# Products of constants in the waits at the borders between sublayers of an encoder trunk

## The reference, cut to what matters

```python
def rmsnorm(x, gain):
    y = xf * lax.rsqrt(jnp.mean(xf * xf, axis=-1, keepdims=True) + EPS)
    return y * gain

def swiglu(h, w_in, w_out):
    gate, up = jnp.split(h @ w_in, 2, axis=-1)
    return (jax.nn.silu(gate) * up) @ w_out

x = x + 0.5 * rmsnorm(swiglu(rmsnorm(x, g[0]), ffn_w_in[l, 0], ffn_w_out[l, 0]), g[1])
...
x = x + rmsnorm(m, g[3])
```

## Time and profile before

| | us |
|---|---|
| median of 3 runs | 2142.0 (2140.52 to 2144.03) |
| the profiled execution | 2141.13 |
| its span, first to last instruction | 2139.3 |
| TensorE busy | 2062.4 (96% of the span) |
| VectorE, ScalarE, GpSimd busy | 900.7, 689.9, 664.4 |
| mean granted clock of TensorE over the span | 0.984 |

### The profile page before, as it was taken

The page is one execution under the profiler, slowest core; times in us unless marked ns, Lnnn a source line. Parts: engine busy times, 40 slices in busy tenths (PEclk is TensorE's granted clock), DMA queues, the critical chain, the costliest instruction groups (busy, mean ns, idle before and its releaser), DMA issues.

```text
span 2139.3 us, 31272 instructions
## 1 busy us (share of the span) xinstructions
PE 2062.4 (96%) x12648; PEld 1695.4 (79%) x12648; DVE 900.7 (42%) x1222; ACT 689.9 (32%) x925; POOL 664.4 (31%) x286
## 2 busy tenths in 40 slices
PE   6999999989989999998999999999999889999997
PEld 5888888767878888887888888778888778888885
DVE  4433331668454333115433311564754766333213
ACT  4222222445342222224222222453543343222221
POOL 2444444230214444441444444100000013444442
PEclk9999999999999999999999999999999999999998
DMA  4223333210122223332222333221211122222332
GB/s 148 87 90 98 96 92 97 89 50 1 59 80 89 97 89 96 98 95 85 88 94 93 96 97 95 87 71 61 71 61 60 51 69 79 98 90 97 93 100 74
DMA packets 51643, 179.61 MB, mean 84 GB/s; under 512 B 5728, under 2 KB 5984, under 8 KB 51552
## 3 DMA queue, kind: packets, MB, share of 16 engines
q1 hardware_dynamic: 51552, 178.30, 25.8%
HBM read 176.18 MB, written 2.10 MB: 83 GB/s over the span
## 4 chain that ended last, share of the span: by engine, by line
PE 93%; DVE 3%; ACT 2%; issue 1%; DMA 0%; SPq 0%; DVEq 0%; ACTq 0%
PE psum L546 28%; PE psum L547 28%; PE psum L548 27%; PE psum L782 1%; PE psum L758 1%; PE psum L886 1%; PE psum L771 1%; PE psum L632 1%; PE psum L935 1%; DVE xt L1530 0%; DVE t_a L1525 0%; DMA const<-consts 0%; PE psum L950 0%; PE psum L762 0%; PE psum L761 0%
## 5 line engine op out<-in xcount | busy, mean ns | idle before, releaser
L498 POOL TENSOR_TENSOR w_lo<-raw,w_hi 128x1024 fp32r<-128x1024 f32 (+1 forms) x282 | 664.1, 2356 | 1443.0 <-ACT w_hi L1134 1442.9
L546 PE MATMUL psum<-xg_hi,w_hi 128*128 128x512 f32 x1896 | 757.5, 400 | 39.8 <-DMA const<-consts 16.2
L547 PE MATMUL psum<-xg_lo,w_hi 128*128 128x512 f32 x1896 | 749.3, 395 | 0.2 <-issue 0.2
L548 PE MATMUL psum<-xg_hi,w_lo 128*128 128x512 f32 x1896 | 747.5, 394 | 0.0
L1134 ACT ACTIVATE w_hi<-raw 128x1024 fp32r<-128x1024 f32 (+1 forms) x339 | 350.9, 1037 | 861.6 <-DMA raw<-w_up 468.0
L546 PEld LDWEIGHTS psum<-xg_hi,w_hi 128*128 128x128 f32 x1896 | 360.0, 190 | 122.8 <-DVE xg_lo L1536 17.4
L548 PEld LDWEIGHTS psum<-xg_hi,w_lo 128*128 128x128 f32 x1896 | 359.9, 190 | 80.3
L547 PEld LDWEIGHTS psum<-xg_lo,w_hi 128*128 128x128 f32 x1896 | 360.6, 190 | 76.4 <-issue 0.7
L546 PE MATMUL psum<-hid_hi,w_hi 128*128 128x512 f32 x704 | 273.9, 389 | 0.0
L547 PE MATMUL psum<-hid_lo,w_hi 128*128 128x512 f32 x704 | 273.9, 389 | 0.0
L548 PE MATMUL psum<-hid_hi,w_lo 128*128 128x512 f32 x704 | 273.9, 389 | 0.0
(11 more groups left out here) (183 smaller groups left out, 1326.6 us busy)
## 6 DMA issues: line engine op xcount, KB each, us to landing
raw<-w_up SPq DMA_DIRECT2D x176, 512.0 KB, 3.3
raw<-w_down SPq DMA_DIRECT2D x64, 512.0 KB, 3.5
raw<-w_hgrn SPq DMA_DIRECT2D x48, 512.0 KB, 3.3
raw<-w_down SPq DMA_DIRECT2D x32, 384.0 KB, 3.2
raw<-w_mla SPq DMA_DIRECT2D x19, 512.0 KB, 3.3
xt<-x_t SPq DMA_DIRECT2D x8, 256.0 KB, 6.8
out<-xt SPq DMA_DIRECT2D x8, 256.0 KB, 2.0
sq<-positions SPq DMA_DIRECT2D x1, 256.0 KB, 9.6
```

The costliest lines, as they stand in the source:

```text
L498: pool.tensor_tensor(w_lo[slot][:, 0:n], raw[slot][:, 0:n], w_hi[slot][:, 0:n].bitcast(F32), ALU.subtract).then_inc(w_ready, 1)
L546: first = pe.matmul(ps, w_hi[slot][:, at:at + n], hi, start=start, stop=False)
L547: pe.matmul(ps, w_hi[slot][:, at:at + n], lo, start=False, stop=False)
L548: return first, pe.matmul(ps, w_lo[slot][:, at:at + n], hi, start=False, stop=stop)
```

## The change

A helper keep_clock(times) issues products of the identity (stationary) with the 256 columns of constants that hold the identity and the ones, plain f32, into bank 7. Nothing reads them. It is called with 1 between the two halves of post_statistics, with 1 before the wait for recip_made, and with 6 behind widen. The statistics at the very end get the first of these only.

```diff
+WHILE_SQUARE, WHILE_ROOT, WHILE_CHUNK = 1, 1, 6
...
+        IDLE_BANK = 7
...
                     if b == 0:
                         close(first)
+                keep_clock(WHILE_SQUARE)
                 pe.wait_ge(sq_ready, squared.next(KB))
...
+            def keep_clock(times):
+
+                for _ in range(times):
+                    pe.matmul(psum[:, IDLE_BANK, 0:2 * P], ident, const[:, 0:2 * P], start=True, stop=True)
...
             for s, (kind, _, _, _) in enumerate(SUBLAYERS):
                 if s:
                     post_statistics()
+                    keep_clock(WHILE_ROOT)
                     pe.wait_ge(recip_made, recips.next())
                     widen()
+                    keep_clock(WHILE_CHUNK)
```

## The result

| | before | after |
|---|---|---|
| median of six, us | 2141.6 (2140.1 to 2144.0) | 2130.0 (2127.6 to 2130.4) |
| ratio | | 0.9941 (95% interval 0.9931 to 0.9952) |
| profiled execution: time, span | 2141.1, 2139.3 | 2130.1, 2128.3 |

The changed kernel is 11.6 us (0.5% by the medians) faster. The forecast was 7.0 us faster, 2135.0, with a range from 2131.5 to 2140.5.

A forecast was written before the change was run, and what follows sets the result against it. TensorE was the bound, losing time at half clock at five borders. Three fifths of 8.6 us (all kept) and two fifths of 3.0 (all dropped) gave 6.4, put at 7.0: 2142.0 − 7.0 = 2135.0, range 2131.5 to 2140.5.

The forecast's parts named there:

- What bounds it: Whole kernel: TensorE, busy 96%; filling waits alone gains nothing, the loss is work at half clock behind the five borders.
- The price of a product and the three fillings: Border waits: 0.43 us a product at held clock, 0.87 otherwise; one, one and six fit, leaving 0.6 us of the third.
- What borders 2 to 5 bring when held: Borders 2 to 5 at full clock: gains of 1.8, 3.0, 1.4 and 1.8 us, 8.0 together.
- Border 1: Entry of the attention layer, bound by its chunks: only 0.2 us there and 0.46 of widening, 0.6 us if held.
- Three borders in five are kept: All five borders: the filler holds the clock at three, depending on how soon after the last wide product the drop falls due.
- The value where it falls: Borders still dropping: full clock returns sooner, worth 0.8, 0.5, 0.6 and 1.0 us at borders 2 to 5, 0 at 1.
- No DMA, no other engine's instruction and no wait moves: Program outside the fillings: the change only adds 41 products on TensorE; no term was counted for the gated layer's inside.
- The end: Last statistics: one filler product of the 41 stands there; no gain was counted for it.
- A: Rival: the clock drops at every border and only comes back sooner; 3.0 us faster, 2139.0; chance 0.14, near mixtures included.
- B: Rival: products of constants don't hold the clock and delay the real ones; 4.6 to 8.6 us slower, 2148.6; chance 0.11.
- C: Rival: all five borders kept, 8.6 us faster, 2133.4; upper part of the forecast, chance 0.70 together with it.
- D: Rival: nothing happens, as filling costs what the clock gives; within 2 us of 2142; chance 0.05.

The follow-up runs named there:

- thin: The changed kernel with each filler product cut from 256 columns to one, same instruction count: median 2141.2 us, ratio 0.9991 to the kernel before.
- twelve: The changed kernel with twelve products behind the widening in place of six: 2141.9 us, ratio 1.0000 to the kernel before.
- not_first: The changed kernel without the root's and the chunk's filler products at the first border: 2132.5 us, ratio 0.9960 to the kernel before.
- after_again: The changed kernel, unchanged, measured a second time: 2128.2 us.
- chunk_only: The changed kernel with only the six products behind the widening, neither of the two early ones: 2135.2 us, ratio 0.9958 to the kernel before.
- more_waits: The changed kernel plus seven products in an attention-layer wait and five ahead of the gated layer's output projection: 2127.8 us, ratio 0.9941 to the kernel before.
- more_waits_again: The changed kernel with the same two further places filled (seven and five products), measured once more: 2130.1 us, ratio 0.9940 to the kernel before.
- shifted: The changed kernel with five wide and nine one-column products in the third wait instead of six wide: 2135.6 us, ratio 0.9974 to the kernel before.
- moved: The changed kernel with 32 one-column products more in the attention layer and its first chunk wait: 2136.3 us, ratio 0.9975 to the kernel before.

## Why the prediction was right and wrong

Between the forecast gain of 7.0 and the spans' 11.0 lie 3.6 us in the gated layer, 0.9 at borders 2 to 5 (7.9 where 7.0 was forecast for all), 0.5 at the end, and −0.9 at border 1 and the start. The medians are 11.6 apart. The borders and the end alone, 7.9 − 0.7 + 0.5 = 7.6 us, would have come close to the 7.0, in part by luck: too few borders were taken as held, but border 1, whose 0.6 was counted, cost 0.7. Without the gated layer's 3.6 us the time would be 2133.6, inside the range.

**What bounds it: right.** The waits go from 25.0 to 6.9 us, and thin, which shortens them too (the last from 15.9 to 5.6 us), gains nothing worth the name at any border (0.04 us at most). The clock was the thing to look at.

**The price of a product and the three fillings: right.** 0.43 was assumed, twelve's 5.0 us for twelve give 0.42. 0.6 us of cover were expected behind the six, 0.59 is there.

**What borders 2 to 5 bring when held: right.** 1.8 + 3.0 + 1.4 + 1.8 = 8.0 was the sum, 1.77 + 2.87 + 1.42 + 1.82 = 7.9 was measured.

**Border 1: wrong by a little.** 0.6 was expected, and three traces give −0.7, +0.4 and +0.4 against the one of before, whose own repeat differs by 0.4. That chunks bind there was right: 10.2 us at half clock or 3.4 make a difference of 0.4 at most (not_first, after_again).

**"Three borders in five are kept": wrong, the smaller of the two steps that failed.** Borders 2 to 5 were kept in each of three traces. Border 1 was kept in the first alone, and it is the one with nothing to gain. Pauses of 0.19, 0.26 and 0.59 us are there and the clock is 1.00. The rule that I weighed against it, from the Trainium skill, page "TensorE: Matmul & The Clock Gate", section "A second HAM failure mode: psum-queue depth-cycling" (short, frequent pauses make the clock go back and forth), is not borne out at these four borders. At border 4 of not_first, with the same first two pauses, the clock did fall. The edge is near, as I had said: with the early two left out (chunk_only) four borders fell, and in not_first and more_waits, with the full filling, seven of twelve did. What failed is that I took the moment of each drop in the trace of before as a sign of whether it would still come. This step and the next took 8.6 to 7.0.

**The value where it falls: wrong in size.** 0.5 us was put on a border of the third kind; fallen for 3.4 us, border 3 of more_waits gained 2.4. The step that failed is that full clock comes back as long after the filler's start as it did after the first real product's: it came 3.4 us after the drop. But the same fall for 6.8 us gains nothing (chunk_only) or loses 1.3 (more_waits_again), so there is no one value. Over the seven fallen borders of not_first and the two more_waits the mean gain is 1.2 us (from −1.3 to 2.4), where the forecast's four values average 0.7. It didn't matter for the result, as none of the four fell.

**What was not in the sum at all: the step that took the time out of the range.** 3.6 of the 11.0 us are from the gated layer. I took "No DMA, no other engine's instruction and no wait moves" to mean that nothing else moves, so the rest of the program stood in the sum at nothing. The list of TensorE's waits, which I had read, had two lines without a releaser, 2.1 and 1.0 us, in this layer. I had even used the stretch 1679.8:1683.2 with the loss of the clock behind it as a sign of where the edge is, and not asked what its pause was: the 2.07 us without a releaser. In the place of that nothing, the runs showed 2.0 us less of waits and 1.5 us less of half-speed work behind the second one. The 32 products ahead of that layer, 128 instructions, move all the code behind them on TensorE's queue. With all borders kept, 8.6 us was the top of my range, with 2 us for the spread of the runs; a term of some us belonged into its width (the 17 traces of this layer lie between 366.6 and 373.8). The gain hangs on this number of products: at 64 nothing is gained (shifted, moved).

**The end: a small term left out.** The last filler was taken at nothing. The clock fell 5.0 us after the last statistics instead of 3.4 (2114.6 − 2109.6, 2123.6 − 2120.2), and the end is 0.46 us shorter.

**The rivals.** A (drops everywhere and comes back sooner) describes border 1 in two of three traces, where it fell for 3.4 us instead of 10.2. B (constants don't hold the clock) is refuted by the four borders at 1.00. C's borders, with the gated layer's 3.6, are what happened. Of D's kind is twelve: filling costs exactly what the clock gives.

## What to carry to other kernels

Where TensorE waits a few microseconds at a border, look at the granted clock behind the wait before the wait itself: here 7.9 us lay in half-speed work behind 25 us of waits, and wide products of constants, on data long there, got them back, when they stood in all three waits and ended before the real operand came. It is no guarantee: with the same filling the clock fell at 7 borders of 12 in three kernels that differ elsewhere. Keep the filler shorter than the wait (six or seven products of 0.43 us in 3.2 us go with a gain of 11 us, twelve with none). And when an edit adds instructions to a queue that runs straight through, compare the waits without a releaser of both traces and repeat the kernel with as many instructions that do nothing, before the time is put down to the edit's idea.

## What the runs showed of the hardware

- Plain f32 products of constants that are nearly all zeros, 256 columns wide, held TensorE's granted clock at 1.00 at 12 borders of 12 in three traces, where it had been 0.50 for 6.8 to 10.2 us; with one column in their place it fell at all five borders in both traces.
- TensorE's waits without a releaser in the gated layer belong to a place in the code: with 8 products more ahead (four instructions each) the wait of 2 us came 32 records earlier, and with 64 more it was back at the same record. The profile has instructions arrive in pieces of 16 KB (68 packets, 1.11 MB), and one of them ends 1.4 or 1.5 us before TensorE goes on. That it ran out of instructions there is the reading that fits; no view shows it directly. Where many products are very short (64 in 1.4 us), such waits were up to 2.6 us long.
- The clock can also fall without any pause of TensorE: 12 one-column products from 414.72 to 417.32, and half clock at 418.20, in one trace of this kernel and not in its two repeats.
